# Order of one expert's weight refill in a four-slot mixture-of-experts loop

## What is computed

```
group_logits = xf @ w_group + b_group            # 8 groups, the best one is taken
e_logits     = (xf @ w_router + b_router)[group] # 8 experts of that group
top_vals, top_loc = top_k(e_logits, 2)           # two experts for each token
for each of 64 experts e, on the tokens that chose it (xb):
    yb = (silu(xb @ w1[e]) * (xb @ w3[e])) @ w2[e]
out = rmsnorm(h + sum of each token's two yb, weighted)
```

## Time and profile before

| | |
|---|---|
| median of three runs | 2086.33 us (2085.6 to 2088.24) |
| profiled execution, its own time | 2089.14 us |
| span of its instructions | 2087.3 us |
| PE busy | 1720.7 us (82%) |
| DVE, ACT and POOL busy | 27%, 19%, 19% |
| read from and written to DRAM | 480 MB and 34 MB |
| SP's queue (q1) | 461.37 MB, 55.8% of the 16 engines' span |
| expert loop | from about 1040 to 2044 us of the span |

### The profile page before, as it was taken

One profiled execution on the slowest core, in us unless ns is written; L12 is line 12 of the kernel. 1 busy time (PEld: TensorE's weight loads), 2 busy tenths in 40 slices (PEclk: granted clock), 3 DMA queues, 4 the chain that ended last, 5 costly groups with the idle time before them and its releaser, 6 DMA issues.

```text
span 2087.3 us, 38809 instructions
## 1 busy us (share of the span) xinstructions
PE 1720.7 (82%) x13684; PEld 928.6 (44%) x13685; DVE 559.9 (27%) x1273; ACT 402.1 (19%) x914; POOL 402.0 (19%) x506
## 2 busy tenths in 40 slices
PE   7999999999999999999576767775777777767564
PEld 4576556644444444455343434443434444434332
DVE  5619223541122322356610111110101111111105
ACT  4011313411211111111111211121211221111113
POOL 1961001172151241001110111110111111101003
PEclk9999999999999999999698989898878989979877
DMA  6320411001110110472699999999999999999996
GB/s 203 151 60 9 151 41 46 21 21 41 50 41 31 61 31 30 162 293 95 275 374 416 412 409 409 406 403 416 412 405 418 405 376 416 409 408 413 420 398 256
DMA packets 96099, 511.10 MB, mean 245 GB/s; under 512 B 30304, under 2 KB 48736, under 8 KB 70944
## 3 DMA queue, kind: packets, MB, share of 16 engines
q1 hardware_dynamic: 79744, 461.37, 55.8%
q0 software_dynamic: 8864, 27.02, 3.5%
q10 hardware_dynamic: 7440, 22.04, 2.7%
HBM read 479.97 MB, written 34.35 MB: 246 GB/s over the span
## 4 chain that ended last, share of the span: by engine, by line
PE 54%; DMA 36%; issue 4%; DVE 4%; POOL 1%; POOLq 1%; ACT 0%; ACTq 0%; SPq 0%; DVEq 0%
DMA gain_b<-xf_rows,gather_idx 18%; DMA tokens<-expert_token_table 16%; PE act_bank L1078 14%; PE act_bank L848 13%; PE dve_bank L1078 6%; PE dve_bank L1144 5%; PE act_bank L1243 5%; PE dve_bank L855 3%; PE act_bank L1255 2%; PE dve_bank L848 1%; DMA unit<-in_w_in 1%; DVE unit L1580 1%; PE act_bank L855 1%; PE dve_bank L1255 1%; PE dve_bank L1061 1%
## 5 line engine op out<-in xcount | busy, mean ns | idle before, releaser
L855 PE MATMUL dve_bank<-ident,gain_b 32*128 32x32 f32 x808 | 75.9, 238 | 225.3 <-DMA gain_b<-xf_rows,gather_idx 213.4
L1243 PE MATMUL act_bank<-unit,gain_a 128*32 128x256 f32 x3200 | 195.0, 398 | 26.8 <-issue 26.2
L2062 DVE TENSOR_TENSOR gain_a<-gain_a,act_bank 128x128 f32<-128x128 f32 x100 | 28.7, 287 | 695.9 <-ACT gain_a L1491 681.4
L1255 PE MATMUL act_bank<-unit,gain_a 128*32 128x256 f32 x2368 | 182.9, 461 | 14.2 <-DVE gain_a L2064 11.6
L855 PEld LDWEIGHTS dve_bank<-ident,gain_b 32*128 32x128 f32 x808 | 66.6, 156 | 270.3 <-issue 270.3
L1491 ACT ACTIVATE gain_a<-act_bank 128x128 f32<-128x128 f32 x101 | 28.0, 278 | 819.9 <-PE act_bank L1243 804.3
L1078 PE MATMUL act_bank<-norm_store,unit 128*128 128x512 f32 x384 | 168.7, 592 | 0.0
L797 POOL COPY gather_idx<-tokens 32x1 int32 x100 | 17.7, 177 | 753.8 <-DMA gain_b<-xf_rows,gather_idx 508.0
L1243 PEld LDWEIGHTS act_bank<-unit,gain_a 128*32 128x32 f32 x3200 | 106.1, 116 | 119.5 <-issue 62.2
L1078 PE MATMUL act_bank<-unit,unit 128*128 128x512 f32 x288 | 127.5, 592 | 0.0
L802 POOL DMA_INDIRECT gain_b<-xf_rows,gather_idx x101 | 94.0, 931 | 125.3 <-PE dve_bank L855 107.5
(11 more groups left out here) (315 smaller groups left out, 2050.6 us busy)
## 6 DMA issues: line engine op xcount, KB each, us to landing
unit<-in_w SPq DMA_DIRECT2D x112, 2048.0 KB
norm_store<-in_w SPq DMA_DIRECT2D x32, 2048.0 KB
mid_store<-in_w SPq DMA_DIRECT2D x32, 2048.0 KB
rows_store<-in_w SPq DMA_DIRECT2D x16, 2048.0 KB
unit_results<-side ACTq DMA_DIRECT2D x100, 128.0 KB, 6.2
unit<-in_w_gate SPq DMA_DIRECT2D x12, 1024.0 KB, 5.1
unit<-in_w_in SPq DMA_DIRECT2D x4, 2048.0 KB, 8.3
unit_results<-unit POOLq DMA_DIRECT2D x4, 2048.0 KB, 13.4
```

What stands on the lines that cost most here:

```text
L855: ins = nc.tensor.transpose(bank[:, n * rows:(n + 1) * rows], block_, ident[0:rows, 0:rows])
L1243: ins = nc.tensor.matmul(act_bank[0][h * CAP:(h + 1) * CAP, 0:2 * FQ].rearrange("t (w n) -> t w n", w=2), xT[:, k], w13[s][:, :, k, h * FQ ...
L1255: ins = nc.tensor.matmul(y_bank[s][z * CAP:(z + 1) * CAP, 0:DQ], hidT[:, j], w2s[s][:, j, z * DQ:(z + 1) * DQ], start=j == 0, stop=j == QU ...
L2062: v.tensor_tensor(hid, silu_g, act_bank[0][:, FQ:2 * FQ], ALU.mult).then_inc(per_slot["hid_ready"][s], 1)
```

## The change

The two calls in `refill` that ask for up and for down weights change places, and the wait for the old expert's last down product, which stood between them, now stands before both.

```diff
                 sp.wait_ge(per_slot["hid_ready"][s], first)
                 sp.dma_start(tokens[:, s], table_of[bass.ds(chosen_expert, 1)].rearrange("e p n -> (e p) n")
                              ).then_inc(tokens_loaded[s], 16)
-                expert_up(up, s)
                 sp.wait_ge(per_slot["y_ready"][s], first)
                 expert_down(down, s)
+                expert_up(up, s)
```

## The result

The changed kernel takes 2095.45 us, the median of 7 runs (2091.32 to 2098.65), against 2086.67 us of the kernel before in the same series (2084.98 to 2088.88). The ratio on record is 1.0037, with a 95% interval of 1.0027 to 1.0046: slower, by 7.7 us (5.6 to 9.6); the medians lie 8.8 us apart. The profiled execution of the kernel after took 2098.65 us, with a span of 2096.9 us. That is 9.6 us more than the span before, but it is also the slowest of the 7. So the profile tells where the time went, and the runs how much it is.

A forecast was written before the change was run, and what follows sets the result against it. The prediction took the DMA queue's weight loads, not PE, to bound the expert loop. Its terms 4.5 + 2.4 + 0.5 = 7.4 us on a base of 2086.3 gave 2093.7 us, range 2089 to 2100.

The forecast's parts named there:

- the first refill: Place 4's refill: the queue is empty, weights go out only after the old down product, 4.5 us later.
- the thin place: Place 43's refill, with 8.9 us of work left in the queue before: a 1.6 us margin remains, counted as 0.5 us.
- the tail: Loop's end: place 63's up weights land last, so its up product and what follows start 2.4 us later.
- the list grid: Expert loop: token lists land every 15.1 to 16.5 us as the queue works off earlier places; this sets the end.
- T(63): The landing of place 63's token list, at 2017.56 us before; T(p) is the same for place p.
- The rival that priced the pause at 6.9 us: At place 43 the queue runs dry for good, 6.9 us more: 2100.1 us, chance 0.16.
- The free tail: At place 63 the mean of the engines counts for the up weights, tail costs nothing: 2091.3 us, chance 0.10.
- The delay taken up later: The pause at 1676 to 1684 us absorbs the first refill's delay, only the tail is left: 2088.7 us, chance 0.12.

The follow-up runs named there:

- the run with both turns as before: The change in places 8 to 59 alone, first and last turn of refills asking as in the kernel before: 2086.65 us, ratio 1.0001.
- the wait alone: The change, but with up weights asked for ahead of down, both waits still before all weight DMAs: 2091.04 us, ratio 1.0021.
- place 4 alone: The kernel before, with only the refill of place 4 asking as in the change: 2089.89 us, ratio 1.0017.
- the kernel with the last turn as before: The change, except that the refills of places 60 to 63 ask as in the kernel before: 2091.69 us, ratio 1.0026.
- the filled kernel: The change with PE's last turn written out and 8 unused matmuls ahead of place 63's up product: 2091.68 us, ratio 1.0029.

## Why the prediction was right, and where it was off

It said 2093.7 us, 7.4 more than before, of which 4.5 at the first refill, 2.4 at the end and 0.5 at the thin place.

Its mechanism held: an idle queue at the first refill, up weights that land last at place 63, and nothing between. That the total came so close, 7.4 us for 7.7 by the ratio, is in part luck, since the tail's term was too small, while the thin place's 0.5 us didn't come: in the one profile of the change the same parts add up to 8.2 us, and in the other kernels the start's cost is 3.3 to 5.4 us and the tail's 1.3 to 3.1.

- *The queue bounds the loop, and the list grid is its clock.* Right. T(63) - T(8) lies between 899.2 and 903.5 us in the kernel before, the change and all experiments, whatever PE does between. Waits for up weights in the middle are free: the run with both turns as before has 58 us of them.
- *The first refill, 4.5 us.* Right in place and size: 4.4 us in the profile. That T(8) lands at 1121.0 and not at 1119.7 is the 1.4 us of the stages ahead. The term is no constant, though. It is the time from the last hid to the end of the old down product, and this was 5.0 us in the change, 6.3 and 6.4 in the wait alone and place 4 alone, and 4.6 to 4.8 in three others; T(8) came 3.3 to 5.4 us late with it, at the top beyond the 5 us that the prediction gave as an end. The granted clock from 1048 to 1052 us, with the down product of place 0, was 0.50 in the wait alone and 1.00 in the kernel with the last turn as before, the 1.2 and the 2.4 GHz level. This, and the tail, may be why the change's 7 runs spread over 7.3 us and the 7 of before over 3.9; no run settles it, and 32 runs of the kernel before in the next series spread over 6.9.
- *The thin place, 0.5 us.* Not contradicted, and too small to be told. SP issued place 43's weights at 1696.39, the share fell to 0.20 between 1688 and 1696 us, and ten places took 165.3 us in place of 163.0 from T(37) to T(47). But from T(47) to T(63) it took 258.4 in place of 260.4. From T(37) to T(63) the change is 0.35 us longer, which is nothing: this stretch took 421.6 to 425.4 us in the six kernels whose refill of place 43 waits as in the change and in which POOL waited for place 37's list, and 420.9 to 423.4 in the seven others. The rival that priced the pause at 6.9 us is out. It counted the mean of the engines, and the bytes show what became of it. The pause took 4.3 us of all engines' time before and 10.4 in the change. Of the 11 MB that stand behind T(63), SP's queue (q1) then moved 6.36 MB in the kernel before, and 8.37 MB in the change, in the 26.3 us up to the gain's landing:

```profile
q1 hardware_dynamic: 1419, 6.36, 59.9%
```
```profile
q1 hardware_dynamic: 1556, 8.37, 77.3%
```

So the engines on average were some 4.6 MB ahead of the queue's order at T(63) before, and 2.6 MB in the change. Most of the longer pause was taken out of this lead, and the gain landed at the same 26.3 us.

- *The tail, 2.4 us.* This is the term that was mis-sized. The wait is as predicted: the up product starts 15.0 us behind its list, not 12.6. But two further things happen, and neither stood in the sum. First, the product that follows the wait may run slower. It took 6.51 us in the change, and 4.97, 5.35, 3.66 and 3.66 in four experiments with this tail (one of them with the added matmuls), against 4.04 before. At 6.51 the granted clock was 0.50 from 2032 to 2040 us, the lower level of 1.2 GHz. I had priced the wait and not the clock behind it. Second, the kernel before had 0.4 us to spare at the picks, which is taken off. The up product starts 2.38 us later and takes 2.47 longer, and 0.41 is to spare. So the tail costs 4.4 us in the profile of the change, where the sum had 2.4, and 1.3 to 3.1 us in the others.
- *The free tail* is out: place 63's up product starts 14.8 to 15.0 us after T(63) in all five kernels with this tail, each time out of a wait for the up weights. The Trainium skill's rule that a semaphore is full only when each engine that takes part has landed its data ("DMA: Bandwidth & Descriptors", "Why a DMA increments its semaphore by 16 and not by 1") agrees with this trace.
- *The delay taken up later* is out as well: T(63) is 5.4 us later in the change, of which 1.4 are from ahead of the loop.

What stays open is how much of the tail's cost in the timed runs is the clock. The profiles have the up product between 0.4 us shorter and 2.5 us longer than before, the timed comparisons can't resolve it, and the filled kernel's clock was up before its filling began. Why the clock came back within the wait in one kernel and 6 us behind it in the change is not shown either.

## What to carry to other kernels

Where a queue holds much more work than the delay, asking later is free (here up to some 5 us, with 30 us or more queued); the cost of a later ask was paid where the queue was empty, and that of a changed order where it ended. So look at the first and the last request, not at the sixty between: here two refills carried 7.1 of 7.7 us. In a refill, ask first for what is consumed first, at least for the last one. And when a wait is put ahead of the last matmuls, price also the clock they will run at.

## What the runs showed of the hardware

- A 128 KB store that ACT issued 22.8 to 24.6 us after T(63), while the last loads of SP's queue were landing, landed 26.6 us after T(63) in five kernels, 0.3 us behind the last load, and took 1.99 to 3.85 us. With the loads done it took 1.95. It does not wait for every load ahead of it: issued 18.1 us after T(63) it landed in 4.6 us, 3.5 us before the last load, and next to 4.7 MB of fresh loads in 5.58 us, 5.4 us before the last.
- By bytes, the 16 DMA engines on average were some 4.6 MB ahead of the order of the full queue in the kernel before; at its 413 GB/s that is some 11 us (an estimate). A pause of 10.4 us in place of 4.3 lowered this to 2.6 MB, and moved the end by 0.35 us, which is within the spread.
- The float32 matmuls of the 128x128 identity on 128 columns took 0.23 us each in a row at 2.4 GHz (44 in 10.09 us, 30 in 6.96 us).
